# Ends of four attention stages: where the first output products, the first weight casts and the modulation rows stand

## The chip, the core and the metric

The kernel runs on one core of a Trainium2 chip. A core has TensorE (PE in the profile, its weight loads PEld), VectorE (DVE), ScalarE (ACT), GpSimd (POOL) and SyncE (SP). Each engine takes its instructions in the order in which they are written and waits on semaphores where the code says `wait_ge`. The metric is the device time of one execution in microseconds; a time is the median of several runs.

## The reference

Two blocks run one after the other on 256 tokens of width 1024. The first (neighbourhood attention with context, Fourier and convolution mixing, 32 experts) is not touched. The second has four layers, i = 0 to 3, of three kinds of attention:

```python
for i in range(4):
    mod = silu(c) @ ada_w[i] + ada_b[i]
    sh1, sc1, g1, sh2, sc2, g2 = split(mod, 6)
    h = rms_norm(x, norm_gain[i, 0]) * (1 + sc1) + sh1
    y = (stick_breaking, moba, sliding_window)[i % 3](h)      # ends in merge_heads(o) @ w_out
    x = x + g1 * y
    h = rms_norm(x, norm_gain[i, 1]) * (1 + sc2) + sh2
    x = x + g2 * ((silu(h @ w_gate) * (h @ w_up)) @ w_down)
```

So layers 0 and 3 are stick-breaking ("sb"), layer 1 is MoBA, layer 2 sliding-window attention ("swa"). There are 16 heads of 64, worked through as 8 pairs. The change lies where the last pairs' attention ends and the product with `w_out` begins.

## The kernel before

Everything on chip is transposed: a tile is 128 channels x 256 tokens, and x, the attention output and y have 8 such tiles each. All orders are written out by hand, one program per engine, and nothing is planned at run time.

**Split products.** To keep float32 accuracy with the fast fp32r type, a weight and an activation are split in two: high (a cast) and low (what is left). ScalarE casts the high part of a weight tile (128x1024, `cast_out`, `cast_piece`, shown as L1462); VectorE subtracts it in place from the ring buffer, which leaves the low part (`low_out` L2472, `low_piece` L2445, `split` L2724). `high_product` (L696) multiplies a high weight with the high and low activations side by side (512 columns), `low_product` (L700) the low weight with the high activation (256 columns); `split_product` (L686) does the same in three products of 256 columns. Weights come by SyncE's transfers (L520) into a ring of three slots.

**A pair.** In sb: scores, then VectorE adds the mask and scale (`zm_ready`), ScalarE runs three activations (L1766, L1768, L1770), VectorE and ScalarE form two halves of the result (L2516, L2524), TensorE sums suffixes (`sb_suffix`, L1148, L1150), VectorE subtracts (`weigh`, L2497), ScalarE takes the exponent (`exponent`, L1750), TensorE multiplies with the values (`sb_output`, L1139) into bank 3, ScalarE casts the high part of that (`mixed`, semaphore `o_ready`) and VectorE forms the low one (`low_mix`, L2478, semaphore `o_low`). In MoBA and swa: scores (L1219, L1309), maxima (L2563 on, L2642 on), exponents (L1812, L1888), scaling (`moba_scale` L2578, `swa_scale` L2656 on), transposes (`moba_turn` L1230, `swa_turn` L1316), copies of the transposes to the work buffer, and the output (`moba_output` L1241, `swa_values` L1327), with the same cast and `low_mix`. Bank 3 holds one pair's output, so pair j's output waits for the `low_mix` of pair j - 1. Swa also projects (L1292) and rotates (`swa_rotate`, L1302) one query tile per pair.

**The output product.** `out_proj` makes tiles 0 to 3 from the first weight chunk (banks 4 to 7, high and low products, L696 and L700) and tiles 4 to 7 from the second (banks 0 to 3, L686). Each tile sums over the 8 pairs, k = 0 to 7. Before the change, tile 0's high products for k = 0 to 6 ran first, then the last pair's output (`last_output`), then k = 7 and everything else, tile after tile. The casts of tiles 2 and 3 (into `xn_parts`) stand on ScalarE behind the last pair's cast, and the subtractions for them on VectorE behind the last `low_mix`. After tile f of the first chunk is done (`y_done`), VectorE adds it to x (`update`, L2113 and L2116), ScalarE casts tile f of the second chunk and VectorE subtracts it; further on come the modulation vectors (`take_mods`), the first feed-forward weights, the squares for the norm, and the last four updates. The norm (L652, L654, L2016, L2018) waits for the last of them.

**Modulation rows.** `group_rows(paired(i), "pairs")` multiplies three chunks of `ada_w` with c (L782, 32 products each; in layer 3 the third is a sum, L801) into banks 0 and 2. ScalarE copies them out after the attention (`group_out`), and GpSimd sends them by DMA (L615) to where VectorE takes them.

Of the kernel before, what the change touches and what calls it, by code (L numbers as in the profile page):

```python
# [14 lines left out]
KT = D // P  # L15
T = 256
# [8 lines left out]
PAIRS = D // (2 * HD)  # L25
# [8 lines left out]
RING = 3  # L34
# [38 lines left out]
FIRST = {}  # L73
# [6 lines left out]
def build(nc, ins, out):  # L80
# [3 lines left out]
    with ctx:  # L84
# [312 lines left out]
        def paired(i):  # L397

            return PAIRED + i
# [237 lines left out]
        def _(pe):  # L637
# [75 lines left out]
            def out_proj(i, last_output=None):  # L713

                for c in range(2):
                    n = FIRST[f"out_{i + 1}"] + c
                    for f in range(4):
                        if (c, f) == (1, 0):
                            pe.wait_ge(ada_taken, paired(i) + 1)
                        x = [(mix_hi[:, k, :], mix_lo[:, k, :]) for k in range(KT)]  # L720
                        hi_k, lo_k = ([t[:, k, :] for k in range(KT)] for t in (w_out_hi[f], part["w_gu"](n, f)))
                        if c == 0:
                            pe.wait_ge(attn_hi, out_splits(i) + f + 1)
                            for k in range(KT):
                                if (f, k) == (0, KT - 1):
                                    if last_output:
                                        last_output()
                                    pe.wait_ge(o_low, PAIRS * (i + 1))
                                high_product(bank[4 + f], hi_k[k], x[k], k == 0)
                        pe.wait_ge(attn_lo, out_splits(i) + 4 * c + f + 1)  # L730
                        for k in range(KT):
                            if c == 0:
                                m = low_product(bank[4 + f], lo_k[k], x[k], k == KT - 1)
                            else:
                                m = split_product(bank[f][:, 0:T], (hi_k[k], lo_k[k]), x[k], k == 0, k == KT - 1)
                        m.then_inc(y_done if f < 3 else used[n % RING], 1)
                        if (i, c, f) == (0, 1, 1):
                            spread_row()
# [347 lines left out]
            def rest():  # L1086
# [3 lines left out]
                for i in layers:  # L1090
# [75 lines left out]
                    def sb():  # L1166
# [18 lines left out]
                        sb_output(PAIRS - 2)  # L1185
                        sb_suffix(PAIRS - 1)

# [57 lines left out]
                    def moba():  # L1245
# [23 lines left out]
                        group_rows(paired(i), "pairs", 0, 2)  # L1269
                        moba_turn(PAIRS - 2)  # L1270
                        group_rows(paired(i), "pairs", 2)
                        moba_output(PAIRS - 2)
                        moba_turn(PAIRS - 1)
# [57 lines left out]
                    def swa():  # L1331
# [8 lines left out]
                        for j in range(1, PAIRS + 2):  # L1340
                            if j < PAIRS:
                                swa_query(j, 0, KT // 2)
                            if j <= PAIRS:
                                swa_rotate(j - 1)
                            if j >= 3:
                                swa_values(j - 3)
                            if j < PAIRS:
                                swa_query(j, KT // 2, KT)
                            if j <= PAIRS:
                                swa_scores(j - 1)  # L1350
                            if j == PAIRS + 1:
                                group_rows(paired(i), "pairs", 1)
                            if j >= 2:
                                swa_turn(j - 2)
                            if j == PAIRS:
                                group_rows(paired(i), "pairs", 0, 1)
                            if j < PAIRS:
                                swa_square_sum(j)

# [6 lines left out]
                    pe.wait_ge(o_low, PAIRS * (i + 1) - 1)  # L1366
                    out_proj(i, {"sb": lambda: sb_output(PAIRS - 1), "swa": lambda: swa_values(PAIRS - 1), "moba": lambda: moba_output(PAIRS - 1)}[KINDS[i]])
# [90 lines left out]
        def _(act):  # L1458
# [262 lines left out]
            for i in layers:  # L1721
# [17 lines left out]
                def sb():  # L1739
# [17 lines left out]
                    for j in range(PAIRS + 1):  # L1757
                        if j >= 3:
                            mixed(j - 3)
                        if j < PAIRS - 1:  # L1760
                            cast_piece(i, V_PIECES + 2 * (j + 1))
# [23 lines left out]
                    cast_out(0, 0)  # L1785
# [42 lines left out]
                def moba():  # L1828
# [4 lines left out]
                    for g in range(FOURS):  # L1833
# [21 lines left out]
                        if g < FOURS - 2:  # L1855
                            cast_piece(i, at + 8)
                    moba_exp(PAIRS - 2)
                    cast_out(0, 0)
                    moba_exp(PAIRS - 1)
                    moba_taken(PAIRS - 2)  # L1860
                    cast_out(0, 1)
# [30 lines left out]
                def swa():  # L1892
# [6 lines left out]
                    for j in range(1, PAIRS + 3):  # L1899
                        if j == PAIRS + 1:  # L1900
                            cast_out(0, 0)
# [3 lines left out]
                        if j == PAIRS + 1:  # L1905
                            cast_out(0, 1)
# [155 lines left out]
        def _(dve):  # L2062
# [398 lines left out]
            for i in layers:  # L2461
# [120 lines left out]
                def moba():  # L2582
# [30 lines left out]
                    moba_scale(PAIRS - 2)  # L2613
                    low_out(0, 0)
                    moba_scale(PAIRS - 1)
# [49 lines left out]
                def swa():  # L2665
# [18 lines left out]
                    for j in range(1, PAIRS + 2):  # L2684
                        if j <= PAIRS:
                            swa_turned(j - 1)
                        if j >= 2:
                            swa_scale(j - 2)
                        if j == PAIRS + 1:
                            low_out(0, 0)  # L2690
# [279 lines left out]
```

## Time and profile before

| what | value |
|---|---|
| median of 3 runs | 1966.45 us (1963.29 to 1967.11) |
| profiled execution | 1966.52 us, its span 1964.3 us |
| TensorE busy | 1757.6 us (89%) |
| VectorE busy | 1185.9 us (60%) |
| ScalarE busy | 855.7 us (44%) |
| chain that ended last | PE 64%, DMA 22%, DVE 10%, ACT 3% |
| mean granted TensorE clock | 0.972 |

Busy time is what an engine's records cover; the chain of waits goes back from the last instruction, at each step to what released it. The granted clock is the share of full speed that the chip gave TensorE. The DMA part of the chain belongs to the first block. The four attention stages end at about 779, 1114, 1420 and 1744 us.

### The profile page before, as it was taken

To read this page: it belongs to the slowest core of one execution; us is meant where nothing else is said; L and a number is where in the kernel's file an instruction comes from. 1 tells how busy PE (TensorE), PEld (TensorE's weight loads), DVE (VectorE), ACT (ScalarE), POOL (GpSimd) and SP (SyncE) were. 2 spreads that over 40 slices of the span, in tenths; PEclk is the share of its full clock that TensorE was granted. 3 is DMA by queue.
4 is the path that set the end of the run, shared out by engine and by line. 5 is a ranking of instruction groups with operands and counts; after the bars stand their busy time and mean duration, and the time that the engine had idled before them with its cause. 6 is when DMAs were issued, how large, how long until landed. Compare 5 with 4: busy or idle time off the path is not lost.

```text
span 1964.3 us, 32850 instructions
## 1 busy us (share of the span) xinstructions
PE 1757.6 (89%) x13662; PEld 1431.1 (73%) x13662; DVE 1185.9 (60%) x2062; ACT 855.7 (44%) x1531; POOL 56.6 (3%) x96
## 2 busy tenths in 40 slices
PE   6999867767767899999999899998999999999998
PEld 4898534434434588888888788887688888988887
DVE  1885201101101487888868888884788886787664
ACT  2565100000000367655445565544565544766552
POOL 0200000000000001000000000000000000000000
PEclk9999989989989899999999999999999999999999
DMA  9788999999999964787763377683178776324533
GB/s 402 286 287 321 403 429 429 427 429 429 429 428 428 410 251 173 284 314 272 270 251 129 112 293 290 255 312 148 60 279 320 269 272 242 134 100 171 206 139 122
DMA packets 42627, 550.31 MB, mean 280 GB/s; under 512 B 5520, under 2 KB 5904, under 8 KB 8080
## 3 DMA queue, kind: packets, MB, share of 16 engines
q1 hardware_dynamic: 34992, 452.13, 58.0%
q0 software_dynamic: 7520, 96.56, 13.0%
q8 instruction: 83, 1.36, 0.3%
q14 instruction: 32, 0.26, 0.0%
HBM read 547.53 MB, written 1.05 MB: 279 GB/s over the span
## 4 chain that ended last, share of the span: by engine, by line
PE 64%; DMA 22%; DVE 10%; ACT 3%; issue 1%; SPq 0%; ACTq 0%; DVEq 0%
PE bank L696 23%; PE bank L686 15%; PE bank L700 12%; DMA ring<-in_moe 10%; DMA ada_ring<-in_moe_side 9%; PE bank L1010 2%; PE bank L671 2%; DVE ring_parts L2472 1%; DMA ring<-in_v 1%; DMA ada_ring<-in_ada_last 1%; DVE ring_parts L2724 1%; PE bank L782 1%; PE bank L1292 1%; PE bank L1163 1%; PE bank L1148 1%
## 5 line engine op out<-in xcount | busy, mean ns | idle before, releaser
L700 PEld LDWEIGHTS bank<-acts,ring_parts 128*128 128x128 f32 x2120 | 298.8, 190 | 23.0
L700 PE MATMUL bank<-acts,ring_parts 128*128 128x256 f32 x2120 | 314.5, 282 | 0.0
L696 PE MATMUL bank<-acts,mixT_parts 128*128 128x512 f32 x1032 | 262.6, 394 | 8.1 <-DVE acts L2786 8.1
L696 PEld LDWEIGHTS bank<-acts,mixT_parts 128*128 128x128 f32 x1032 | 184.3, 189 | 44.6 <-DVE acts L2786 12.8
L2403 DVE TENSOR_TENSOR mixT<-mixT,bank 128x128 f32<-128x128 f32 x32 | 9.2, 288 | 339.4 <-ACT mixT L1671 339.4
L686 PE MATMUL bank<-acts,ring_parts 128*128 128x256 f32 x728 | 204.9, 281 | 0.0
L1462 ACT CAST mixT_parts<-ring 128x1024 fp32r<-128x1024 f32 (+1 forms) x144 | 143.3, 1000 | 80.2 <-PE bank L700 78.3
L696 PE MATMUL bank<-acts,xn_parts 128*128 128x512 f32 x640 | 160.3, 392 | 0.0
L686 PEld LDWEIGHTS bank<-acts,ring_parts 128*128 128x128 f32 x728 | 138.0, 190 | 0.0
L696 PEld LDWEIGHTS bank<-acts,xn_parts 128*128 128x128 f32 x640 | 115.1, 189 | 20.6
L2300 DVE CUSTOM_DVE_ANT_0 ada_ring<-ada_ring,c_row 128x1024 f32<-128x1024 f32 x108 | 127.2, 1220 | 0.0
L2724 DVE TENSOR_TENSOR ring_parts<-ring,mixT_parts 128x1024 fp32r<-128x1024 f32 x80 | 98.0, 1224 | 46.7 <-ACT mixT_parts L1462 46.7
L686 PE MATMUL bank<-acts,w_out_hi 128*128 128x256 f32 x680 | 125.2, 284 | 0.0
L1671 ACT ACTIVATE mixT<-bank 128x128 f32<-128x128 f32 x32 | 8.9, 278 | 258.6 <-PE bank L1010 258.6
L1010 PE MATMUL bank<-ada_ring,xsq 128*32 128x256 f32 x1024 | 75.7, 446 | 46.3 <-DMA ada_ring<-in_moe_side 46.3
L1462 ACT CAST xn_parts<-ring 128x1024 fp32r<-128x1024 f32 x98 | 102.7, 1054 | 10.1 <-PE bank L700 10.1
L1010 PE MATMUL bank<-ring,xsq 128*32 128x256 f32 x1024 | 66.1, 403 | 45.5 <-DMA ring<-in_moe 44.7
L686 PEld LDWEIGHTS bank<-acts,w_out_hi 128*128 128x128 f32 x680 | 105.6, 190 | 1.0 <-DVE ring_parts L2445 0.4
L1462 ACT COPY work<-bank 128x256 f32<-128x256 f32 (+2 forms) x132 | 53.0, 423 | 118.7 <-PE bank L700 95.3
L1010 PEld LDWEIGHTS bank<-ada_ring,xsq 128*32 128x32 f32 x1024 | 34.1, 125 | 86.3 <-DMA ada_ring<-in_moe_side 62.2
L1462 ACT COPY mixT<-bank 128x256 f32<-128x256 f32 x66 | 24.5, 373 | 163.2 <-PE bank L1040 156.9
L1462 ACT CAST w_out_hi<-ring 128x1024 fp32r<-128x1024 f32 x77 | 80.4, 1049 | 32.9 <-PE bank L686 26.2
(433 smaller groups left out, 3321.1 us busy)
## 6 DMA issues: line engine op xcount, KB each, us to landing
ring<-in_moe SPq DMA_DIRECT2D x48, 2048.0 KB, 27.2
ada_ring<-in_moe_side SPq DMA_DIRECT2D x48, 2048.0 KB, 25.9
ada_ring<-in_ada POOLq DMA_DIRECT2D x45, 2048.0 KB, 10.2
ring<-in_gu SPq DMA_DIRECT2D x44, 2048.0 KB, 9.0
ring<-in_down SPq DMA_DIRECT2D x32, 1408.0 KB, 6.1
ring<-in_qk SPq DMA_DIRECT2D x12, 2048.0 KB, 8.5
ring<-in_out SPq DMA_DIRECT2D x9, 2048.0 KB, 8.1
ring<-in_na SPq DMA_DIRECT2D x8, 2048.0 KB, 9.2
```

The lines of the kernel that those rows point to most:

```text
L671: m = mm(dst, w[:, k, lo:lo + P], h[:, k, :], start=k == 0, stop=k == KT - 1)
L686: m = mm(dst, w[a], x[b], start=start and (a, b) == (0, 0), stop=stop and a == 1, skip_group_check=shared)
L696: mm(dst[:, :], w, both(*x), start=start, stop=False)
L700: return mm(dst[:, 0:T], w, x[0], start=False, stop=stop)
L782: m = mm(dst[32 * q:32 * q + 32, :], c[:, kk, :], w[:, kk, q % 2 * T:(q % 2 + 1) * T], start=k == 0, stop=k == 3)
L1010: m = mm(bank[0][CAP * q:CAP * (q + 1), 0:T], xg[:, 4 * c + k, h * CAP:(h + 1) * CAP], w[:, k, q * T:(q + 1) * T], start=(c, k) == (0, 0), ...
L1148: mm(bank[6 + h][:, 0:TRI], tri_parts[:, 0, :], half[:, h, :], start=n == 0, stop=False, skip_group_check=True)
L1163: m = mm(bank[4 + h][:, a:b], qk[hp, keys], qk[hp, tokens], start=True, stop=True)
L1292: m = mm(bank[j % 2][:, 0:T], w[:, k, j % 4 * P:(j % 4 + 1) * P], hT[:, k, :], start=k == 0, stop=k == KT - 1)
L1462: return nc.scalar.copy(o, i)
L2300: r = V.tensor_tensor_reduce(w, w, c2_row[:, :], 1.0, 0.0, ALU.mult, ALU.add, mod[:, d:d + 1])
L2724: m = V.tensor_tensor(part["w_gu"](n, f), full["w_gu"](n, f), gu_hi(step, f).bitcast(F32), ALU.subtract)
```

## The change

`out_proj` is cut into `out_high(i, f, k0, k1)` and `out_low(i, f, k0, k1)`, so that parts of a tile can be issued elsewhere, and tile 1's high products stand in front of tile 0's last step. Part of tile 0 is issued among the last pairs' steps: in sb three high products ahead of the last suffix sum and the rest behind it, in MoBA four between the last two outputs, in swa six ahead of the last transposes. In MoBA the transposes of pair 7 move ahead of pair 6's output. The last pair's output then comes after tile 0's low products for k = 0 to 6 in sb and swa, and before its remaining high ones in MoBA. The first casts of the output weight (`cast_out`) stand earlier on ScalarE, `low_out(0, 0)` later on VectorE in MoBA and earlier in swa, and the modulation rows go ahead of the transposes of pairs 6 and 7 in MoBA and one pair step earlier in swa. The number of products, casts and transfers stays as it was. The diff, with most unchanged lines left out:

```diff
@@ -710,32 +710,42 @@
...
-            def out_proj(i, last_output=None):
-
-                for c in range(2):
-                    n = FIRST[f"out_{i + 1}"] + c
-                    for f in range(4):
-                        if (c, f) == (1, 0):
-                            pe.wait_ge(ada_taken, paired(i) + 1)
-                        x = [(mix_hi[:, k, :], mix_lo[:, k, :]) for k in range(KT)]
-                        hi_k, lo_k = ([t[:, k, :] for k in range(KT)] for t in (w_out_hi[f], part["w_gu"](n, f)))
-                        if c == 0:
-                            pe.wait_ge(attn_hi, out_splits(i) + f + 1)
-                            for k in range(KT):
-                                if (f, k) == (0, KT - 1):
-                                    if last_output:
-                                        last_output()
-                                    pe.wait_ge(o_low, PAIRS * (i + 1))
-                                high_product(bank[4 + f], hi_k[k], x[k], k == 0)
-                        pe.wait_ge(attn_lo, out_splits(i) + 4 * c + f + 1)
-                        for k in range(KT):
-                            if c == 0:
-                                m = low_product(bank[4 + f], lo_k[k], x[k], k == KT - 1)
-                            else:
-                                m = split_product(bank[f][:, 0:T], (hi_k[k], lo_k[k]), x[k], k == 0, k == KT - 1)
-                        m.then_inc(y_done if f < 3 else used[n % RING], 1)
-                        if (i, c, f) == (0, 1, 1):
-                            spread_row()
+            def out_high(i, f, k0, k1):
+
+                pe.wait_ge(attn_hi, out_splits(i) + f + 1)
+                for k in range(k0, k1):
+                    pe.wait_ge(o_low, PAIRS * i + k + 1)
+                    high_product(bank[4 + f], w_out_hi[f][:, k, :], (mix_hi[:, k, :], mix_lo[:, k, :]), k == 0)
+
+            def out_low(i, f, k0, k1):
+
+                n = FIRST[f"out_{i + 1}"]
+                pe.wait_ge(attn_lo, out_splits(i) + f + 1)
+                for k in range(k0, k1):
+                    m = low_product(bank[4 + f], part["w_gu"](n, f)[:, k, :], (mix_hi[:, k, :], mix_lo[:, k, :]), k == KT - 1)
+                if k1 == KT:
+                    m.then_inc(y_done if f < 3 else used[n % RING], 1)
+
+            def out_proj(i):
+
+                out_high(i, 1, 0, KT - 1)
+                out_high(i, 0, KT - 1, KT)
+                out_low(i, 0, KT - 1, KT)
+                out_high(i, 1, KT - 1, KT)
+                out_low(i, 1, 0, KT)
+                for f in range(2, 4):
+                    out_high(i, f, 0, KT)
+                    out_low(i, f, 0, KT)
+                n = FIRST[f"out_{i + 1}"] + 1
+                pe.wait_ge(ada_taken, paired(i) + 1)
+                for f in range(4):
+                    pe.wait_ge(attn_lo, out_splits(i) + 4 + f + 1)
+                    for k in range(KT):
+                        m = split_product(bank[f][:, 0:T], (w_out_hi[f][:, k, :], part["w_gu"](n, f)[:, k, :]), (mix_hi[:, k, :], mix_lo[:, k, :]),
+                                          k == 0, k == KT - 1)
+                    m.then_inc(y_done if f < 3 else used[n % RING], 1)
+                    if (i, f) == (0, 1):
+                        spread_row()
@@ -1183,7 +1193,12 @@
...
                         sb_output(PAIRS - 2)
+                        pe.wait_ge(sk["zm_ready"], base + PAIRS)
+                        out_high(i, 0, 0, 3)
                         sb_suffix(PAIRS - 1)
+                        out_high(i, 0, 3, KT - 1)
+                        out_low(i, 0, 0, KT - 1)
+                        sb_output(PAIRS - 1)
@@ -1266,11 +1281,14 @@
...
                             moba_scores(g)
-                        group_rows(paired(i), "pairs", 0, 2)
+                        group_rows(paired(i), "pairs")
                         moba_turn(PAIRS - 2)
-                        group_rows(paired(i), "pairs", 2)
+                        moba_turn(PAIRS - 1)
                         moba_output(PAIRS - 2)
-                        moba_turn(PAIRS - 1)
+                        out_high(i, 0, 0, 4)
+                        moba_output(PAIRS - 1)
+                        out_high(i, 0, 4, KT - 1)
+                        out_low(i, 0, 0, KT - 1)
@@ -1340,8 +1358,12 @@
...
                                 swa_query(j, 0, KT // 2)
+                            if j == PAIRS:
+                                group_rows(paired(i), "pairs", 0, 1)
                             if j <= PAIRS:
                                 swa_rotate(j - 1)
+                            if j == PAIRS + 1:
+                                group_rows(paired(i), "pairs", 1)
                             if j >= 3:
@@ -1349,13 +1371,15 @@
...
                             if j == PAIRS + 1:
-                                group_rows(paired(i), "pairs", 1)
+                                pe.wait_ge(sf["s_ready"], base + PAIRS)
+                                out_high(i, 0, 0, KT - 2)
                             if j >= 2:
                                 swa_turn(j - 2)
-                            if j == PAIRS:
-                                group_rows(paired(i), "pairs", 0, 1)
                             if j < PAIRS:
                                 swa_square_sum(j)
+                        out_high(i, 0, KT - 2, KT - 1)
+                        out_low(i, 0, 0, KT - 1)
+                        swa_values(PAIRS - 1)
@@ -1363,8 +1387,7 @@
...
                         moba()
-                    pe.wait_ge(o_low, PAIRS * (i + 1) - 1)
-                    out_proj(i, {"sb": lambda: sb_output(PAIRS - 1), "swa": lambda: swa_values(PAIRS - 1), "moba": lambda: moba_output(PAIRS - 1)}[KINDS[i]])
+                    out_proj(i)
                     n0 = FIRST[f"gu_{i}"]
@@ -1757,6 +1780,8 @@
...
                             mixed(j - 3)
+                        if j == PAIRS:
+                            cast_out(0, 0)
                         if j < PAIRS - 1:
@@ -1782,7 +1807,6 @@
...
                             group_out(2, "step")
-                    cast_out(0, 0)
                     mixed(PAIRS - 2)
@@ -1854,11 +1878,11 @@
...
                             cast_piece(i, at + 8)
+                    cast_out(0, 0)
+                    cast_out(0, 1)
                     moba_exp(PAIRS - 2)
-                    cast_out(0, 0)
                     moba_exp(PAIRS - 1)
                     moba_taken(PAIRS - 2)
-                    cast_out(0, 1)
                     moba_high(PAIRS - 2)
@@ -1897,13 +1921,11 @@
...
                     for j in range(1, PAIRS + 3):
-                        if j == PAIRS + 1:
-                            cast_out(0, 0)
                         if j >= 3:
...
                             copy(mix_hi[:, j - 3, :], bank[3][:, 0:T]).then_inc(sf["o_ready"], 1)
-                        if j == PAIRS + 1:
-                            cast_out(0, 1)
+                        if j in (PAIRS, PAIRS + 1):
+                            cast_out(0, j - PAIRS)
                         if j < PAIRS:
@@ -2611,8 +2633,8 @@
...
                     moba_scale(PAIRS - 2)
+                    moba_scale(PAIRS - 1)
                     low_out(0, 0)
-                    moba_scale(PAIRS - 1)
                     low_mix(sf, PAIRS - 1, PAIRS - 2)
@@ -2684,10 +2706,10 @@
...
                             swa_turned(j - 1)
+                        if j == PAIRS + 1:
+                            low_out(0, 0)
                         if j >= 2:
                             swa_scale(j - 2)
-                        if j == PAIRS + 1:
-                            low_out(0, 0)
                         if j >= 3:
```

## Rows read from the trace of the kernel before

**Rows 1.** Chain of waits, end of layer 0: start us, us, what

```profile
775.73 1.03 DVE work L2497 x2
...
777.68 0.90 PE bank L1139 x8
...
779.95 2.36 DVE ring_parts L2472 x2
```

**Rows 2.** Chain of waits, end of layer 1

```profile
1113.28 0.82 PE bank L1241 x8
...
1115.48 2.36 DVE ring_parts L2472 x2
```

**Rows 3.** Chain of waits, end of layer 2

```profile
1407.11 1.58 PE bank L1309 x8
...
1412.71 3.59 PE bank L782 x64
...
1418.75 0.82 PE bank L1327 x8
```

**Rows 4.** Chain of waits, end of layer 3

```profile
1742.28 0.82 PE bank L1139 x8
```

**Rows 5.** Timeline of TensorE: start, us, instructions, [idle before <- what ended it]

```profile
775.53 1.85 PE L696 MATMUL bank<-acts,w_out_hi 128*128 128x512 f32 x7
...
779.82 1.12 PE L700 MATMUL bank<-acts,ring_parts 128*128 128x256 f32 x8
...
1099.54 3.66 PE L782 MATMUL bank<-ada_ring,c_wide 128*32 128x256 f32 x64
1105.29 1.24 PE L1230 MATMUL bank<-const_sb,work 128*128 128x128 f32 x6 [2.09 <-DVE work L2578]
1106.46 3.19 PE L782 MATMUL bank<-ada_ring,c_wide 128*32 128x256 f32 x32
...
1136.15 0.40 PE L686 MATMUL bank<-acts,first_gu_hi 128*128 128x256 f32 x2
...
1404.79 0.70 PE L1302 MATMUL bank<-qn,const_sb 128*128 128x256 f32 x2 [1.79 <-DVE qn L2625]
...
1738.84 0.62 PE L1148 MATMUL bank<-sp_parts,tri_parts 128*128 128x384 f32 x2 [0.78 <-DVE sp_parts L2524]
```

**Rows 6.** Windows: us, busy us (x instructions) of each engine, granted clock, DMA share, GB/s

```profile
1094.00:1098.00 4.00, 1.93 (x18) 1.12 (x14) 3.93 (x10) 1.83 (x5) 0.00 (x0) 1.00 0.96 410
1105.00:1107.00 2.00, 1.71 (x14) 1.16 (x18) 1.79 (x4) 1.95 (x10) 0.00 (x0) 0.66 0.00 0
1107.00:1109.60 2.60, 2.60 (x34) 1.02 (x26) 0.79 (x2) 1.37 (x3) 0.00 (x0) 0.60 0.00 0
1407.00:1409.70 2.70, 2.70 (x16) 2.20 (x14) 2.08 (x7) 0.37 (x1) 0.00 (x0) 0.55 0.30 127
1115.50:1138.90 23.40, 22.62 (x167) 21.32 (x165) 21.82 (x39) 15.10 (x27) 3.69 (x7) 1.00 0.79 318
```

**Rows 7.** Timeline of ScalarE, layers 0, 1 and 2

```profile
768.37 0.85 ACT L1766 ACTIVATE work<-zm_other 128x768 f32<-128x768 f32 x1 [1.85 <-PE bank L1150]
...
1101.95 0.40 ACT L1812 ACTIVATE work<-work,stat 128x128 f32<-128x128 f32 x1 [4.15 <-DVE stat L2569]
...
1409.91 0.48 ACT L1462 COPY work<-bank 128x384 f32<-128x384 f32 x1 [2.39 <-PE bank L1316]
```

**Rows 8.** Timeline of VectorE, layers 1 and 2

```profile
1106.76 1.03 DVE L2578 TENSOR_TENSOR work<-work,stat 128x256 f32<-128x256 f32 x2
...
1138.85 0.48 DVE L2116 SCALAR_TENSOR_TENSOR xT<-bank,vec_sb,xT 128x256 f32<-128x256 f32 x1
...
1413.24 0.16 DVE L2656 TENSOR_TENSOR stat<-stat 128x4 f32<-128x4 f32 x1 [1.49 <-ACT stat L1890]
```

**Rows 9.** SyncE's queue in layer 1; TensorE's waits from 660 us on, the longest

```profile
1052.30 20.00 SPq L520 DMA_DIRECT2D ring<-in_out  x2
...
PE bank L696 <- DVE acts L2786: 9.5, 12, 1.7
```

## Prediction

> **What bounds the kernel now.** I read the chain of waits first, at the end of each attention stage. In all four it has one shape: the last pair's attention output on TensorE, a copy of it on ScalarE, the cast of weight tile 2, then VectorE's subtraction for tiles 2 and 3 [rows 1 to 4]. From there the chain stays on VectorE. In layer 1 VectorE is busy 21.82 of the 23.40 us that follow [rows 6] and starts its last residual update at 1138.85 [rows 8], while TensorE is through all eight output tiles at 1136.15 [rows 5], 2.7 us before the last update. So TensorE leads there, and a saved TensorE microsecond pays only if it moves the last pair's output. Call that instruction group V7: 777.68, 1113.28, 1418.75 and 1742.28 in layers 0 to 3. After the last update come the norm and the feed-forward products; in the list of TensorE's waits no weight transfer appears after 660 us, and the longest entry is VectorE's [rows 9]. So what V7 or the updates gain should reach the end one for one.
>
> **Prices.** Seven high products take 1.85 us and eight low ones 1.12 us, overlaps included [rows 5]; in a stream that is 0.25 us per high product and 0.14 per low one: three highs 0.75, four 1.0, seven lows 0.98. The cast takes 1.04, tile 0's subtraction 1.22 on VectorE. A modulation chunk is 32 products: two take 3.66, so one 1.83. The same 32 took 3.19 in layer 1 while the granted clock was at its lower level (1.2 GHz for the part that makes the mean 0.60) [rows 5, 6]. The added waits of the high products ask for pairs taken long before; I cost a satisfied one at nothing, hidden under the 0.25 us product ahead of it, and at most some 0.05 us each.
>
> **The earlier casts.** ScalarE is idle 1.85 us in front of the last pair's first activation in layer 0 (layer 3 has the same code), 4.15 before the exponents in layer 1, 2.39 in layer 2 [rows 7]. One cast fits into the first, two (2.0) into the second, one into the third. The weight chunk is there: in layer 1 its two transfers are issued between 1052.30 and 20.00 us later [rows 9], and the cast now comes at 1097.8. Cost nothing; without that cover 1.04 us each.
>
> **Layer 0 (stick-breaking).** Three high products now stand ahead of the last suffix sum, whose input is ready before TensorE is. The sum ends just ahead of the weighing that follows it at 775.73; the exponent and V7 follow at once [rows 1]. All three move by 0.75 and a few hundredths, V7 to 778.45. TensorE's own queue would allow 776.45 + 4 x 0.25 + 0.98 = 778.43, so both agree. TensorE's idle time behind V7 is filled, but the chain goes by ScalarE's copy and VectorE. Price: **+0.77**.
>
> **Layer 3.** Same code, but TensorE waits 0.78 us before the suffix sum [rows 5], and three highs (0.75) fit. After its end at 1740.19 come 1.0 + 0.98, to 1742.17, against an exponent that ends at 1742.14: V7 stays at 1742.2. TensorE ends 1.5 us sooner and then waits for VectorE. **0.0**, within 0.1.
>
> **Layer 1 (MoBA).** Before: TensorE idles 2.09 us to 1105.29, transposes pair 6, runs the third chunk for 3.19 in front of pair 6's output, and seven highs in front of V7 [rows 2, 5]. After: all three chunks run from 1099.54 to 1105.03, inside that idle. Exponents 7 no longer stand behind a cast, and scale 7 no longer behind a subtraction, so scale 7 starts some 0.5 sooner than its 1106.76 [rows 8], ends at 1107.3, and the transposes end at 1108.2. Pair 6's output runs at 1108.15 to 1109.0, its copy to 1109.45, the copy of pair 7's transposes (0.86) to 1110.24. Four highs fill TensorE to 1110.0. V7 at 1110.3, 2.9 earlier. What is late next is tile 0: after V7 (to 1111.1) come three highs 0.75, seven lows 0.98, seven highs of tile 1 1.75, and tile 0's last two products, so it is done at 1115.1, where VectorE, through with tiles 2 and 3 at 1117.84 before [rows 2], would take it at 1114.9. Only then can the cast of the second weight's tile 0 start (1115.15), its subtraction at 1116.25; VectorE alone would be there at 1115.8. So 0.5 of the 2.9 is lost. Later tiles are ready before VectorE asks. **-2.4**.
>
> **Layer 2 (sliding window).** Before: 1.79 us idle ahead of the last rotation, then output, scores and transposes at a lowered clock, a chunk, output 6, two chunks (3.59), transposes, seven highs, V7 at 1418.75 [rows 3, 5]. After: the first chunk fills the idle (1402.95 to 1404.85), so the rotation moves by 0.1 at most. If the clock then stays up, scores end at 1407.6 instead of 1408.69 [rows 3]. The maxima start 0.7 sooner, at 1408.0, and scale 7 ends at 1413.97. Tile 0's subtraction (1.22) goes into the 1.49 us that VectorE waits for the exponents [rows 8]. TensorE: transposes 6 to 1408.7, two chunks to 1412.3, output 6 to 1413.1, six highs to 1414.55, transposes 7 to 1415.4, one high and seven lows to 1416.65, V7 there. **-2.1**; with the old clock about -0.9.
>
> **Sum.** 0.77 - 2.4 - 2.1 + 0.0 = -3.7. The profiled execution took 1966.52 us (span 1964.3 and 2.2 around it), the median of the runs is 1966.45, so both give **1962.8**. About 0.2% (3.9 us) is what a measurement of this kernel can tell from no change, so the forecast lies at that edge.
>
> **The clock.** The granted clock was at a mean of 0.66 and 0.60 in two stretches after the 2.09 us idle, and 0.55 after the 1.79 us one, but stayed at 1.00 in layer 1 with TensorE busy only 1.93 of 4.00 us [rows 6]. Full-clock time lost: 0.34 x 2.0 + 0.40 x 2.6 = 1.7 us in layer 1, at least 0.45 x 2.7 = 1.2 in layer 2. Both idle stretches get filled, so I take no fall. A rule speaks against it: the Trainium skill (TensorE: Matmul & The Clock Gate, Part 4: PE-mode transpose) says that transposes don't count as TensorE activity in the way other matmuls do. By that rule layer 1's new stretch, 1105.03 to 1108.2, of two transpose groups and 1.1 us of idle, is nearly empty, and the clock falls as before. The trace is against it in part, since the stretch at 1.00 above holds transposes too.
>
> **Rivals.**
> (A) The clock still falls once, in layer 1 or 2. Loss up to 1.7 by the two sums above: 1966.5 - 3.7 + 1.7 = **1964.5**. For it: those two falls, and 1.1 us of idle between the transposes of pairs 6 and 7. Against: less idle than before.
> (B) TensorE bounds the output products after all, and VectorE's long row of updates only follows it. Then the gain is how much sooner tile 2 starts: 0.9 in layer 0, 1.5 in layer 3, 2.8 in layer 1, 3.65 in layer 2, together 8.9: **1957.6**. For it: TensorE is busy 22.62 of 23.40 [rows 6]. Against: its 2.7 us lead and the chain.
> (C) The last pair's chain is set by its own softmax, and the early products merely take other idle time: **1966.5**. For it: layer 3. Against: two chunks of 3.59 us that stand in the chain itself in layer 2 [rows 3].
> (D) Slower: TensorE works in order, and what now stands ahead of V7 delays it, as in layer 0. This holds in layers 1 and 2 only at the low clock, where products double (chunk 3.19 for 1.83). In layer 2 two chunks then cost +2.7, six highs, transposes and lows +2.7, against -2.1: +3.3. In layer 1 transposes, output and four highs, doubled in part, take back 1.8 of 2.4: -0.6. With layer 0's +0.8 that is +3.5: **1970.0**. It decides against the change once more than some 7.5 us of these two ends run at half clock, since half of that is the gain. Against: full clock in most of both ends now.
>
> **Chances.** Forecast 0.62, A 0.14, B 0.10, C 0.07, D 0.07. The likeliest gives 1962.8. Half of the forecast's weight, all of B and a little of A (0.02) lie beyond 0.2% faster: 0.43 and, for VectorE gaps that I can't price, 0.45. Slower is D: 0.07. The rest, 0.48, is within 0.2%. The range reaches from 1959.6 (a part of B, runs that spread over 3.8 us) to 1966.8 (A and C).
>
> **What would show it.** Layer 0: V7 0.8 later against the third chunk's end, TensorE without idle behind it. Layer 3: the same distance from suffix sum to V7. Layer 1: 0.3 us of idle before pair 6's transposes, from the first scores' end to V7 10.7 us instead of 13.7. Layer 2: no 1.79 us wait ahead of the last rotation, granted clock 1.00 in both falls' places. From V7 to the last update as before in layers 0, 2 and 3, and 0.5 longer in layer 1. The forecast is wrong if a stage's gain is lost behind V7, if VectorE waits for tiles, or if the clock falls elsewhere.

## The result: slower, and the profile after

| | changed kernel |
|---|---|
| median | 1976.33 us (4 runs, 1974.65 to 1979.54), before beside it 1965.72 |
| ratio to before | 1.0057, 95% interval 1.0040 to 1.0075 |
| profiled execution | 1974.65 us, its span 1972.5 us, mean granted clock 0.968 |
| forecast | 1962.8 us, range 1959.6 to 1966.8 |

The change costs 10.6 us where 3.7 were forecast as gain. Another 11 executions gave 1976.03 us (1974.0 to 1979.76), ratio 1.0046 (1.0030 to 1.0063).

**The ends themselves.** First the chain of waits of the changed kernel (start us, us, what), where its rows answer to [rows 1 to 4]: each last pair's output V7 (L1149 was L1139, L1256 was L1241, L1345 was L1327), and in layer 2 the modulation chunks (L792 was L782).

```profile
778.61 0.90 PE bank L1149 x8
...
1116.69 0.87 PE bank L1256 x8
...
1413.73 3.59 PE bank L792 x64
...
1421.42 0.82 PE bank L1345 x8
...
1749.25 0.90 PE bank L1149 x8
```

Then TensorE's timeline in layers 1 and 2 (columns as in [rows 5]), and windows over the ends of the two layers, in which the clock had fallen before (columns as in [rows 6]):

```profile
1111.75 0.87 PE L1245 MATMUL bank<-const_sb,work 128*128 128x128 f32 x6 [0.36 <-DVE work L2600]
1113.78 0.87 PE L1245 MATMUL bank<-const_sb,work 128*128 128x128 f32 x6 [1.15 <-DVE work L2600]
```

```profile
1105.00:1118.00 13.00, 11.38 (x158) 7.25 (x152) 9.31 (x19) 7.26 (x25) 0.00 (x0) 1.00 0.01 3
1405.00:1421.00 16.00, 15.38 (x167) 10.26 (x166) 12.76 (x39) 9.51 (x29) 0.00 (x0) 1.00 0.36 133
```

The 2.09 us of idle time of layer 1 is down to 0.36, the 1.79 us of layer 2 is gone from its place, and the clock stays at 1.00 (2.4 GHz) through both ends, where it had been at a mean of 0.60 and 0.55 for a while. So far the change does what was forecast.

**Where the time went.** It is lost behind the attention, at the second norm. Its sum needs VectorE's squares (L652, then L654 for the last of them); then follow the first feed-forward products, up to the first of the second step (`second_gu_hi`). (Ahead of the sum stand four of the eight k steps of the first feed-forward tile, called the gained gate here, summed in bank 5; its other four steps stand behind it.) TensorE's timeline of the changed kernel, those three rows in each layer:

```profile
806.02 1.22 PE L652 MATMUL bank<-xsq,const_sb 128*128 128x256 f32 x2 [3.00 <-DVE xsq L2148]
807.32 1.22 PE L654 MATMUL bank<-xsq,const_sb 128*128 128x256 f32 x2
...
824.87 0.85 PE L696 MATMUL bank<-acts,second_gu_hi 128*128 128x512 f32 x3
...
1142.17 0.70 PE L652 MATMUL bank<-xsq,const_sb 128*128 128x256 f32 x2 [1.28 <-DVE xsq L2148]
1143.47 1.22 PE L654 MATMUL bank<-xsq,const_sb 128*128 128x256 f32 x2 [0.60 <-ACT xsq L2008]
...
1157.11 1.08 PE L696 MATMUL bank<-acts,second_gu_hi 128*128 128x512 f32 x4
...
1446.63 0.73 PE L652 MATMUL bank<-xsq,const_sb 128*128 128x256 f32 x2 [2.58 <-DVE xsq L2148]
1447.93 1.22 PE L654 MATMUL bank<-xsq,const_sb 128*128 128x256 f32 x2 [0.57 <-ACT xsq L2008]
...
1464.42 0.88 PE L696 MATMUL bank<-acts,second_gu_hi 128*128 128x512 f32 x3
...
1774.52 0.93 PE L652 MATMUL bank<-xsq,const_sb 128*128 128x256 f32 x2 [2.57 <-DVE xsq L2148]
1775.82 1.22 PE L654 MATMUL bank<-xsq,const_sb 128*128 128x256 f32 x2 [0.37 <-ACT xsq L2008]
...
1789.03 1.31 PE L696 MATMUL bank<-acts,second_gu_hi 128*128 128x512 f32 x5
```

The same rows of the kernel before, in layers 0 and 2 (L652 starts at 1138.52 and 1767.52 in layers 1 and 3, after 0.78 us of idle time in both):

```profile
805.09 0.70 PE L652 MATMUL bank<-xsq,const_sb 128*128 128x256 f32 x2 [1.18 <-DVE xsq L2126]
806.39 0.70 PE L654 MATMUL bank<-xsq,const_sb 128*128 128x256 f32 x2 [0.60 <-ACT xsq L1986]
...
818.45 0.85 PE L696 MATMUL bank<-acts,second_gu_hi 128*128 128x512 f32 x3
...
1443.98 0.70 PE L652 MATMUL bank<-xsq,const_sb 128*128 128x256 f32 x2 [0.77 <-DVE xsq L2126]
1445.29 0.70 PE L654 MATMUL bank<-xsq,const_sb 128*128 128x256 f32 x2 [0.60 <-ACT xsq L1986]
...
1457.35 0.85 PE L696 MATMUL bank<-acts,second_gu_hi 128*128 128x512 f32 x3
```

Two things are to be seen. The idle time in the brackets of L652 has grown by 1.82, 0.50, 1.81 and 1.79 us. And the two products of L654 take 1.22 us instead of 0.70, and from the start of L654 to the second step it takes 17.55, 13.64, 16.49 and 13.21 us, where it was 12.06, 12.08, 12.06 and 12.08. The windows from L654 to that step say why (columns as before; the number ahead of the DMA share is the granted clock). Before:

```profile
806.40:818.40 12.00, 12.00 (x78) 10.93 (x79) 8.45 (x20) 9.54 (x17) 0.00 (x0) 1.00 0.43 183
1445.30:1457.30 12.00, 12.00 (x78) 10.93 (x79) 9.45 (x21) 9.60 (x16) 0.00 (x0) 1.00 0.52 221
```

After:

```profile
807.30:824.80 17.50, 17.48 (x78) 15.88 (x79) 9.69 (x22) 11.66 (x20) 0.00 (x0) 0.66 0.30 127
1143.50:1157.10 13.60, 13.60 (x78) 12.39 (x79) 9.75 (x22) 10.67 (x18) 0.00 (x0) 0.88 0.46 193
1447.90:1464.40 16.50, 16.46 (x78) 15.04 (x79) 9.74 (x22) 10.77 (x18) 0.00 (x0) 0.71 0.39 166
1775.80:1789.00 13.20, 13.18 (x78) 11.98 (x79) 9.67 (x21) 10.27 (x17) 0.00 (x0) 0.91 0.12 52
```

The same 78 products, TensorE busy throughout, at a mean clock of 0.66 to 0.91: part of the stretch runs at 1.2 GHz. In layer 0 the fall begins while TensorE is still idle and lasts long after it works again:

```profile
804.00:805.00 1.00, 0.00 (x0) 0.00 (x0) 1.00 (x3) 0.00 (x0) 0.00 (x0) 1.00 0.92 393
805.00:806.00 1.00, 0.00 (x0) 0.00 (x0) 0.52 (x3) 0.81 (x2) 0.00 (x0) 0.73 1.11 475
...
818.00:819.00 1.00, 1.00 (x5) 0.90 (x4) 0.29 (x1) 1.00 (x2) 0.00 (x0) 0.50 0.00 0
819.00:820.00 1.00, 1.00 (x6) 0.86 (x6) 1.00 (x2) 1.00 (x2) 0.00 (x0) 0.94 0.00 0
```

**The account** closes. From one layer's second step to the next layer's L654 (in layer 0 from the start): +0.93, -2.77, -2.57 and -0.07 us, together -4.5. From L654 to the second step: +5.49, +1.56, +4.43 and +1.13, together +12.6. The difference, 8.1 us, is that of the spans (1972.5 - 1964.3 = 8.2). In the list of waits the same shows as one row (engine, line, waited for: us, times, longest); it was 3.5 us in all four layers before:

```profile
PE bank L652 <- DVE xsq L2148: 9.4, 4, 3.0
```

### The profile page after: what moved, and what is told of

It reads as the page before. It is cut to its first block, busy times and chain, and to the rows that moved or that the text cites. A ratio compares the mean times of both kernels' runs of the same rounds, so it can differ in the third digit from the quotient of the medians.

```text
span 1972.5 us, 32874 instructions
## 1 busy us (share of the span) xinstructions
PE 1762.1 (89%) x13662; PEld 1439.2 (73%) x13662; DVE 1186.4 (60%) x2062; ACT 856.2 (43%) x1531; POOL 56.8 (3%) x96
## 4 chain that ended last, share of the span: by engine, by line
PE 63%; DMA 22%; DVE 10%; ACT 3%; issue 1%; SPq 0%; POOL 0%; ACTq 0%; DVEq 0%
PE bank L696 23%; DMA ada_ring<-in_moe_side 20%; PE bank L686 15%; PE bank L700 12%; PE bank L1020 2%; PE bank L671 1%; DVE ring_parts L2494 1%; DMA ada_ring<-in_ada_last 1%; DVE ring_parts L2746 1%; PE bank L1310 1%; PE bank L792 1%; PE bank L1173 1%; PE bank L1158 1%; DVE ring_parts L2467 1%; PE bank L1149 1%
```

## The experiments

Theory: the output products reach TensorE sooner, but the sum waits for VectorE as before; what TensorE gains gathers into one longer idle stretch ahead of the sum, and there the clock falls. Rivals: the falls belong to the new order in some other way; they were there before in other executions; the order itself is slower.

**1. Fill the stretch.** Ahead of the sum, in the changed kernel:

```diff
 if k == KT // 2:
+    for _ in range({0: 22, 1: 8, 2: 19, 3: 19}.get(i, 0)):
+        mm(bank[5][:, T:2 * T], first_w(0, 0)[0], gained_hi[:, 0, :], start=True, stop=True, ...)
     norm_of_sums(5 + 2 * i)
```

> The changed kernel, with extra products of 256 columns that nobody reads (22, 8, 19 and 19 in layers 0 to 3) on TensorE ahead of the norm's sum, where it waited 3.00, 1.28, 2.58 and 2.57 us. Theory 1 (the longer idle stretch lowers TensorE's clock, and that is the whole loss): the granted clock stays at 1.00 through the norm and the first feed-forward products, the 12.6 us lost there come back, and the time is 1961 to 1963 us. Theory 2 (the new order itself slows what follows, or the clock falls for another reason): at least 1973 us, as without the extra products.

Measured: **1961.65 us**, ratio 0.9974 (0.9960 to 0.9987) to before. The fill and the sum behind it, layer 0:

```profile
804.70 2.73 PE L1423 MATMUL bank<-acts,first_gu_hi 128*128 128x256 f32 x22
807.85 0.70 PE L652 MATMUL bank<-xsq,const_sb 128*128 128x256 f32 x2 [0.42 <-DVE xsq L2150]
```

No fall at this place in any layer, L654 to the second step in 12.06 or 12.07 us again. Some 14 us hang on whether TensorE has products there, more than the whole loss. (This kernel's gained gate lacks the sums of k = 0 to 3; see the last section.)

**2. Make the stretch without the change.** The kernel before leaves out the first four of eight k steps of the gained gate, 12 products ahead of the sum:

```diff
-m = split_product(..., k == 0, k == KT - 1, True)
+if k < 4:
+    continue
+m = split_product(..., k == 4, k == KT - 1, True)
```

> The kernel before, with the first four of the eight steps of the gained gate product left out in all four layers (12 products each, so its result lacks them). They stand right ahead of the wait for the norm's sum, so that wait grows from 0.8 to 1.2 us to about 2.2 to 2.6, with nothing else moved. Theory 1 (idle stretch, then clock): the clock falls there as in the changed kernel, and the kernel becomes slower by 5 to 13 us although it does 5.7 us less TensorE work. Theory 2 (it takes the new order): no slower than the kernel before, 1964 to 1966 us, since the work left out stood in idle time.

Measured: **1973.0 us**, ratio 1.0028 (1.0015 to 1.0041): less work and more time. Layer 2 of it, the sum on TensorE's timeline and the window behind it:

```profile
1444.68 0.67 PE L652 MATMUL bank<-xsq,const_sb 128*128 128x256 f32 x2 [2.29 <-DVE xsq L2128]
```

```profile
1445.90:1462.70 16.80, 16.80 (x79) 15.29 (x80) 9.76 (x22) 10.75 (x18) 0.00 (x0) 0.70 0.38 162
```

There 16.8 us pass at a mean clock of 0.70 for what takes 12.06. The old order with a longer idle stretch does the same, so the new order isn't needed for it.

**3 to 5. The layers' parts alone,** the other layers in the old order. The edit in outline; ScalarE's and VectorE's orders follow the same condition:

```diff
+NEW = (1,)          # experiment 3; (0, 3) in 4, (2,) in 5
...
+if i in NEW:
+    out_proj(i)
+else:
...
+    out_proj_old(i, ...)
```

> Only layer 1 (MoBA) has the new order; the other three are as in the kernel before. Theory 1: 2.8 us gained up to the norm, the idle ahead of the norm grows to about 1.3 and the clock falls for one short stretch as it did in the changed kernel (1.6 us back), so about 1964.5 us; if it does not fall, 1963. Theory 2 (MoBA's part is among the causes of the loss): above 1967.

> Only layers 0 and 3 (stick-breaking) have the new order. Theory 1: no gain ahead of the norm (plus 0.7 in layer 0), the idle there grows to 3.0 and 2.6 us, the clock falls (5.5 and 1.1 us in the changed kernel): 1970 to 1974 us. Rival (the sliding-window layer is what costs, and the earlier layers only pass it on): 1966 us.

> Only layer 2 in the new order, the other three as before. Theory (the second output group of the last pair comes sooner, and then TensorE's longer idle stretch ahead of the norm's sum lets its clock fall): the group about 2.3 us sooner than before, the idle stretch ahead of the sum 2.6 us against 0.8, TensorE at 1.2 GHz for some 10 us after it, the next layer's feed-forward step 2 us later than before; time about 1968 us, 1.001. Rival (the stretch doesn't matter, the loss is made in other layers): the feed-forward step 2.3 us sooner, time 1963.5 us, 0.9988.

Measured: layer 1 alone 1965.68 us (0.9994, 0.9981 to 1.0007), layers 0 and 3 alone **1973.09** (1.0033, 1.0020 to 1.0047), layer 2 alone 1965.85 (0.9999, 0.9985 to 1.0014). Of the three parts only layers 0 and 3 lose measurably; they gain nothing and lengthen the stretch most. But the three ratios add up to 0.26%, some 5 us, where the whole change costs 0.46 to 0.57%: about half of the loss belongs to no part alone. Layers 1 and 2 alone can't be told from the kernel before, and both times lie between the theory and its rival. Layer 1's saving was in its profile, 2.7 us; the same profile has a fall in layer 0, whose code there is the old one and whose idle stretch was 1.16 us (timeline, then the window behind it):

```profile
808.12 0.70 PE L653 MATMUL bank<-xsq,const_sb 128*128 128x256 f32 x2 [1.16 <-DVE xsq L2206]
```

```profile
809.40:826.20 16.80, 16.78 (x78) 15.32 (x79) 9.73 (x22) 11.71 (x20) 0.00 (x0) 0.70 0.31 133
```

So the kernel before stands near the edge itself: with 1.18 us its profiled execution had no fall there, this one had, at 4.7 us. Layer 2's fall was short, 1.3 us, where some 4 were expected: its time missed the theory's 1968 by 2 us, and the rival's 1963.5 by as much.

**6. Only what gains, filled:** layers 1 and 2 in the new order, 8, 8, 19 and 5 products in the free half of bank 4.

> Layers 1 and 2 in the new order, layers 0 and 3 as before, and unread products of 256 columns (8, 8, 19 and 5 of them in layers 0 to 3) ahead of the norm's sum, in the free half of another bank than in the filled kernel before. Theory (the clock falls because TensorE idles there; the order itself saves 2.8 us in layer 1 and 2.4 us in layer 2 and loses 0.7 us in layer 0): no stretch at 1.2 GHz, the sum in layers 1 and 2 as soon as in the changed kernel, layer 0 at its old place; about 1960.5 us, 0.997 or a little less. Rival (the products' gain in the filled kernel came from what they left out of the work): no gain over the changed kernel, 1966 us or more.

Measured: **1960.86 us** (12 runs), ratio 0.9977 (0.9963 to 0.9991), faster than both kernels and with the whole work done. It also rules out that the first fill gained by what it left out.

**7. The control:** the kernel before, with 8, 5, 5 and 5 such products.

> The kernel before with 8, 5, 5 and 5 unread products of 256 columns ahead of the norm's sum. Theory (with 1.2 us and 0.8 us of idle time there it stands at the edge and falls in some of its executions only): 0 to 2 us faster than before, with a narrower spread; the sum's own place unchanged in all four layers. Rival (products ahead of the norm shorten the time in another way than by the clock): faster by 4 us or more, like the changed kernel filled.

Measured: 1966.99 us, ratio 1.0012 (0.9998 to 1.0026). The products give nothing where there is no long stretch to fill, so in 1 and 6 it is the prevented falls and the new order that pay. The expected 0 to 2 us of gain did not come: either the kernel before seldom has a fall at this place, or the products cost something of their own; the run doesn't separate the two.

**8. Instructions or work?** The changed kernel with its 16 two-column products ahead of the sum instead of behind it:

```diff
 if k == KT // 2:
+    shift_product()
     norm_of_sums(5 + 2 * i)
-if k == KT - 1:
-    shift_product()
```

> The changed kernel with its sixteen two-column products of the shift, which stood behind the norm's sum step 7, ahead of the norm's sum instead: the same work, only its place in TensorE's order differs. They cover about 1.2 us of the idle stretch with instructions but with 32 columns of real work. Theory A (what counts is that TensorE has instructions): the recorded idle stretch falls from 3.0 and 2.6 us to about 1.2, fewer falls of the clock, 1962 to 1968 us. Theory B (what counts is the columns that are worked on): the clock falls as in the changed kernel, 1974 us or more.

Measured: 1963.65 us, ratio 0.9993 (0.9978 to 1.0008), 10 to 13 us under the changed kernel (by the ratios or the medians) with only an order changed. But three layers of the profile still had a fall (L654 took 1.22 us in layer 0, behind 1.31 us of idle time). The falls were short, 3.4 us each, and cheap: L654 to the second step took 0.3 to 0.6 us more than in layer 1, where the products covered the whole stretch and none fell. Behind the sum, where those products had stood, TensorE now waits for VectorE, and a fall first eats into that wait. In layer 0, with a fall, and in layer 1, without:

```profile
812.82 0.47 PE L696 MATMUL bank<-acts,first_gu_hi 128*128 128x512 f32 x1 [0.60 <-DVE acts L2115]
...
1143.37 0.47 PE L696 MATMUL bank<-acts,first_gu_hi 128*128 128x512 f32 x1 [1.41 <-DVE acts L2115]
```

Theory A gives the time; B is right that small products don't keep the clock as the filling does.

**9 to 12.** The changed kernel again; with layer 0 alone filled (22 products); filled by about half (11, 4, 9, 9); and layers 1 and 2 in the new order with the edit of experiment 8 in them.

> The changed kernel unaltered. Alone, the layers' parts came to +0.33% (layers 0 and 3), -0.06% (layer 1) and -0.01% (layer 2), together +0.26% or 5 us, where the whole change had +0.57% or 11 us from four executions. Theory A (the parts add up, the four executions fell high): 1970 to 1973 us. Theory B (together they cost more than alone, since each shift of the work changes where the clock falls next): 1974 us or more again.

> The changed kernel with 22 unread products of 256 columns ahead of the norm's sum in layer 0 only. Theory (the fall of the clock behind layer 0's longest idle stretch, 3.0 us, is the largest part of the loss, 5.5 us): no stretch at 1.2 GHz behind it, the feed-forward step 0.7 us later than before instead of 6.2 us, time 5 to 6 us under the changed kernel's beside it. Rival (the clock falls later in the layer all the same, or the other layers' falls grow): less than 2 us under it.

> The changed kernel with about half the filling: 11, 4, 9 and 9 products, so that some 1.7, 0.9, 1.5 and 1.5 us of idle time are left ahead of the norm's sum instead of 3.0, 1.3, 2.6 and 2.6. Theory A (the loss grows with the idle stretch): falls of the clock in some layers, each of 3.4 us and not 10 to 14 us, time halfway, 1963 to 1967 us. Theory B (there is a length from which it always falls and under which never): either as the changed kernel or as the filled one, within 1.5 us.

> Layers 1 and 2 in the new order with their two-column products of the shift ahead of the norm's sum, layers 0 and 3 as before; no unread products. Theory: the norm's sum 2.8 and 2.4 us sooner, an idle stretch of 0 and 0.9 us, at most one short fall of the clock, 0.1 to 1.3 us; 1960 to 1962 us, 0.9975 to 0.9985. Rival (only large products keep the clock): 1965 us, as with layer 2 alone in the new order.

Measured: the changed kernel again 1976.03 us, so the parts don't add up to the whole (theory B); layer 0 filled 1972.99, ratio 1.0034 (1.0016 to 1.0052), 3 us under the changed kernel beside it and not 5.5, between theory and rival; half filled 1969.85, 1.0014 (0.9999 to 1.0030), outside both theories: layers 0 and 1 had no fall, layers 2 and 3 one each at 4.7 us and more; the two layers with their shift products first 1963.1, 0.9987 (0.9970 to 1.0004), which can't be told from the kernel before and lies between theory and rival, though its profile had only the one short fall that the theory allowed, in layer 2, at 0.3 us. With layer 0 filled, the falls behind it were other ones (windows, layers 0 to 3):

```profile
807.90:820.00 12.10, 12.08 (x79) 11.00 (x80) 8.52 (x21) 9.64 (x17) 0.00 (x0) 1.00 0.43 183
1139.80:1156.60 16.80, 16.79 (x78) 15.32 (x79) 9.73 (x22) 10.74 (x18) 0.00 (x0) 0.70 0.37 159
1447.60:1461.30 13.70, 13.68 (x79) 12.48 (x80) 9.77 (x22) 10.80 (x18) 0.00 (x0) 0.88 0.47 201
1771.20:1788.00 16.80, 16.80 (x78) 15.29 (x79) 9.76 (x22) 10.74 (x18) 0.00 (x0) 0.70 0.09 39
```

Layer 1, with the idle 1.28 us of the changed kernel, lost 4.7 us instead of 1.6, layer 3 4.8 instead of 1.1, and layer 2 1.6 instead of 4.4. So a fall's length is no property of its layer, and the cost of one can't be taken out by itself.

**All profiles together:** idle time ahead of the sum, and what L654 to the second step then took beyond 12.07 us, from the profiled execution of each kernel (stretches with two-column products in them left out).

| kernel | layer 0 | layer 1 | layer 2 | layer 3 |
|---|---|---|---|---|
| before | 1.18: 0 | 0.78: 0 | 0.77: 0 | 0.78: 0 |
| changed | 3.00: 5.5 | 1.28: 1.6 | 2.58: 4.4 | 2.57: 1.1 |
| changed again | 2.98: 5.5 | 1.27: 1.5 | 2.58: 4.4 | 2.56: 1.1 |
| gate steps dropped | 2.68: 1.1 | 2.29: 1.3 | 2.29: 4.7 | 2.29: 0 |
| layer 1 only | 1.16: 4.7 | 1.27: 0 | 0.77: 0 | 0.76: 0 |
| layers 0, 3 only | 3.00: 5.6 | 0.77: 0 | 0.77: 0 | 2.56: 1.1 |
| layer 2 only | 1.17: 0 | 0.78: 0 | 2.59: 1.3 | 0.78: 0 |
| layer 0 filled | 0.45: 0 | 1.28: 4.7 | 2.58: 1.6 | 2.58: 4.8 |
| layers 1, 2 with shift first | 1.17: 0 | | | 0.77: 0 |
| half filled | 1.69: 0 | 0.81: 0 | 1.54: 4.8 | 1.53: 4.7 |
| filled; 1, 2 filled; before filled | 0.23 to 0.42: 0 | 0.20 to 0.34: 0 | 0.20 to 0.37: 0 | 0.19 to 0.37: 0 |

Up to 0.81 us of idle time no fall in 24 cases, from 1.16 to 1.28 a fall in 4 of 8, from 1.53 to 1.69 in 2 of 3, from 2.29 on in 14 of 15. What a fall costs doesn't follow the idle time: 1.16 us once cost 4.7 and 2.57 cost 1.1. It follows how long the low clock lasts, by windows of 1 us: 3.4 us in nine of the twenty falls (1.1 to 1.6 us lost), 10.2 us in eight (4.4 to 4.8 lost), 13.7 us in three (5.5 to 5.6 lost).

## Why the prediction was wrong, step by step

**The failed step** is in layer 3, and holds for all four: "TensorE ends 1.5 us sooner and then waits for VectorE. **0.0**". It was costed as free lead of an engine off the chain. Measured, the wait ahead of the norm's sum grew by 1.8 us in layers 0, 2 and 3 and by 0.5 in layer 1, TensorE fell to 1.2 GHz in all four, and this cost 12.6 us in the profiled execution. Experiments 1 and 2 show it from both sides. The prediction looked for falls only inside the ends, where the trace of before showed them; it had seen that V7 gains and loses at other places than TensorE's own end, but never added up where TensorE's saved time would lie. Its last line did name the sign, a clock that falls elsewhere.

The trace of before held the price at another place. At the start of layer 1 TensorE waits 2.81 us for VectorE, and the clock falls behind it; layer 3 has the same wait and a mean clock of 0.57 over 8 us. The wait, the window over it, and the same place in experiment 1, with the same wait:

```profile
999.98 0.77 PE L686 MATMUL bank<-w_out_hi,acts 128*128 128x512 f32 x1 [2.81 <-DVE acts L2094]
...
998.00:1009.00 11.00, 9.02 (x33) 7.27 (x34) 9.41 (x19) 6.70 (x12) 0.00 (x0) 0.84 0.42 167
```

```profile
999.00:1010.00 11.00, 7.91 (x21) 6.02 (x22) 8.28 (x18) 6.75 (x13) 0.00 (x0) 0.69 0.55 212
```

With the stretch filled, the changed kernel ran at 1961.65 us (experiment 1), inside the stated range and 4.2 us under the kernel before beside it. So this one step is what the sum lacked.

**The terms of the sum** were close. Layer 0: V7 0.69 later against the scores ahead of it, forecast 0.77. Layer 3: V7 0.02 sooner, the distance to the norm 25.27 us instead of 25.24 [rows 4], forecast 0.0. Layer 1: V7 3.05 sooner against the last scores ahead of it, forecast 2.9; behind it 0.24 us were lost (25.48 to L652 instead of 25.24 [rows 2]) where 0.5 were priced, since tile 0 was less late than worked out (done 4.56 us behind V7's start, not 4.8). Layer 2: the stage up to the norm 2.57 us shorter, forecast 2.1. Together -4.5 against -3.7.

**The clock inside the ends** came as forecast, 1.00 in both old places. The Trainium skill's rule on transposes (TensorE: Matmul & The Clock Gate, Part 4: PE-mode transpose) would have had the clock fall in layer 1's new stretch: with two transpose groups and idle times of 0.36 and 1.15 us it did not fall in this profile.

**The rivals.** A priced a fall in the same places, 1.7 us, and named the right kind of cost in the wrong place and at a seventh of its size. B and C are ruled out by the terms above. D had the direction, 1970.0, but by products ahead of V7 at the low clock; layers 1 and 2 did gain 2.8 and 2.6 us in full, so its mechanism isn't what happened. Its sentence that some 7.5 us at half clock decide against the change holds, with the place left open: layer 0 alone had more. The range missed because none of its ends held a fall outside the changed stretch.

**Left open:** why a fall is short in one case and long in the next, and which of the stretches between 1.16 and 1.69 us bring one. How much of the 12 to 14 us that executions of the kernel before spread over comes from such falls wasn't settled: with the stretch filled they still spread over 8 us (12 runs against 35). Part of it comes from elsewhere: in four profiles with the same code up to there, layer 0's sum starts between 805.1 and 809.9 us, and the fall at the start of layer 1 shown above lasted 3.4 us in the kernel before and 6.8 in experiment 1. Layers 1 and 2 in the new order, with nothing added or moved, were not run together.

## What to carry to other kernels

An engine's lead is not free when it is TensorE's: add up where the saved time will gather, and if it joins one wait, price a fall of the clock there, here 1.1 to 5.6 us, in 20 of 26 stretches of 1.16 to 3.0 us of idle time. Speeding up the work ahead of a wait that another engine ends pays only as far as it moves that engine; the rest had better stay spread out or be filled with work that can be moved into the wait, as the shift products were (10 to 13 us for an order of instructions). When adopting a change by parts, keep those that move the chain (layers 1 and 2) and leave those that only lengthen the lead (layers 0 and 3), and fill the wait of those kept: only with it did the gain show (experiment 6), while layer 1 or layer 2 alone, unfilled, showed none.

## What the runs showed of the hardware

- A short wait is enough: stretches of 1.16 to 1.28 us without work brought a fall of the clock in 4 of 8 profiled cases, and after a fall it stayed at 1.2 GHz for as long as from 805.5 to 819.1 us in layer 0 of the changed kernel, 13 us of it with TensorE busy. The Trainium skill (TensorE: Matmul & The Clock Gate, Why this matters for your kernels) advises against long idle gaps between bursts of matmuls; these runs agree that idle time does it, but the stretches are shorter than those it warns of.
- Two-column products kept the recorded idle time short but not the clock: behind 16 of them and 0.9 to 1.3 us of idle time it fell in 4 of 4 cases, at 0.3 to 0.6 us each (experiments 8 and 12; in the other two, where they left no idle time, it did not fall).
- In experiment 1 each unread product was written with `start=True` into the free half of the bank in whose other half the gained gate was being summed. The gate's sum then lacked all steps up to there: the output's relative error was the same 0.464 as that of experiment 2, which leaves out those four steps. The same products in another bank left the sum whole. The Trainium skill (PSUM — Partial Sum Buffer, The four PSUM rules) says that the first product of a group clears the marks of its whole bank, not only of the columns it writes; the runs agree.
